# The last five blocks' rows summed on chip, an earlier conditioning piece, and GpSimd on two tiles' gates

## The reference

```python
mod = silu(c) @ w_ada + b_ada                       # 9 rows of 6 pieces of 1024
sh1, sc1, g1, sh2, sc2, g2 = split(mod, 6)
h = x * (1 + sc1) + sh1
z = h @ w_in + b_in                                 # conv, attention, gMLP columns and 3 gates
merged = sig(gA) * A + sig(gB) * B + sig(gC) * C
x = layer_norm(alpha * x + (1 + g1) * (merged @ w_o), ln1_g, ln1_b)
h2 = x * (1 + sc2) + sh2
# 16 experts, top 2 of one group for each token
y = sum(gate[e] * ((silu(h2 @ w_e_gate[e]) * (h2 @ w_e_up[e])) @ w_e_down[e]) for e in chosen)
x = layer_norm(alpha * x + (1 + g2) * y, ln2_g, ln2_b)
```

## Time and profile before

| | us |
|---|---|
| median of three runs | 1091.23 |
| lowest and highest | 1091.19, 1094.38 |
| the profiled execution, its own time | 1096.24 |
| its span in the trace | 1094.1 |
| PE busy | 1001.8 (92%) |
| DVE, POOL, ACT busy | 488.0, 248.1, 189.9 |
| PE busy from 1050.00 to 1094.10 | 0.0 |

### The profile page before, as it was taken

One profiled execution on the slowest core, in us unless ns is written; L12 is line 12 of the kernel. 1 busy time (PEld: TensorE's weight loads), 2 busy tenths in 40 slices (PEclk: granted clock), 3 DMA queues, 4 the chain that ended last, 5 costly groups with the idle time before them and its releaser, 6 DMA issues. The chain is left out here.

```text
span 1094.1 us, 22154 instructions
## 1 busy us (share of the span) xinstructions
PE 1001.8 (92%) x8966; PEld 669.3 (61%) x8966; DVE 488.0 (45%) x1277; ACT 189.9 (17%) x447; POOL 248.1 (23%) x281
## 2 busy tenths in 40 slices
PE   4999999999899999999999999987999999998930
PEld 3777778456676667667777774555655555554510
DVE  2121999973357888855114004677133111110117
ACT  2110112113122213221111110111111111111103
POOL 0000004535121123323335420000212221221133
PEclk8998999999898999999999999987999999999975
DMA  9955645542615205014072308142899899999756
GB/s 298 308 122 149 193 155 173 177 157 89 227 29 157 74 16 193 30 44 121 11 179 71 116 26 331 67 180 100 326 364 378 313 413 388 422 416 419 316 155 125
DMA packets 93732, 214.23 MB, mean 196 GB/s; under 512 B 23464, under 2 KB 48303, under 8 KB 89533
## 3 DMA queue, kind: packets, MB, share of 16 engines
q1 hardware_dynamic: 78388, 186.20, 47.8%
q0 software_dynamic: 6400, 19.01, 5.8%
q10 hardware_dynamic: 8849, 7.64, 2.6%
HBM read 200.46 MB, written 16.92 MB: 199 GB/s over the span
## 5 line engine op out<-in xcount | busy, mean ns | idle before, releaser
L1787 PE MATMUL bank<-arena 128*128 128x288 f32 (+6 forms) x1778 | 445.5, 406 | 8.1 <-DMA arena<-in_w_pa 2.6
L1787 PEld LDWEIGHTS bank<-arena 128*128 128x128 f32 (+2 forms) x1778 | 322.1, 193 | 123.6 <-issue 47.8
L2178 PE MATMUL bank<-arena 128*32 128x256 f32 x3136 | 181.1, 382 | 4.7 <-issue 3.5
L2178 PEld LDWEIGHTS bank<-arena 128*32 128x32 f32 x3136 | 102.3, 109 | 74.8 <-issue 6.7
L1739 DVE TENSOR_TENSOR arena<-arena,bank 128x128 f32<-128x128 f32 x49 | 14.2, 289 | 225.3 <-ACT arena L1176 225.0
L939 POOL DMA_INDIRECT expert_rows<-arena,ints x49 | 47.8, 976 | 224.0 <-ACT arena L1187 224.0
L2197 PE MATMUL bank<-arena 128*32 128x256 f32 x1568 | 94.6, 381 | 0.0
L889 POOL TENSOR_SCALAR arena<-arena 128x288 f32<-128x288 f32 x46 | 43.3, 942 | 212.0 <-ACT arena L1129 212.0
L1249 DVE SCALAR_TENSOR_TENSOR arena<-arena 128x512 f32<-128x512 f32 x120 | 81.9, 742 | 0.0
L1801 PE MATMUL bank<-arena 128*128 128x288 f32 x256 | 69.3, 428 | 2.6 <-DVEq L1267 2.6
L2197 PEld LDWEIGHTS bank<-arena 128*32 128x32 f32 x1568 | 45.9, 108 | 31.8 <-issue 2.0
(11 more groups left out here) (284 smaller groups left out, 888.6 us busy)
## 6 DMA issues: line engine op xcount, KB each, us to landing
arena<-in_w_e_gate SPq DMA_DIRECT2D x16, 2048.0 KB
arena<-in_w_e_up SPq DMA_DIRECT2D x16, 2048.0 KB
arena<-in_w_e_down SPq DMA_DIRECT2D x16, 2048.0 KB
arena<-in_w_ada SPq DMA_DIRECT2D x8, 2048.0 KB, 10.7
arena<-in_w_in SPq DMA_DIRECT2D x8, 2048.0 KB, 10.1
arena<-in_w_ada SPq DMA_DIRECT2D x8, 1024.0 KB, 11.7
arena<-in_x_prompt SPq DMA_DIRECT2D x8, 512.0 KB, 7.1
arena<-in_w_in SPq DMA_DIRECT2D x14, 256.0 KB, 8.2
```

Source lines behind the costliest of these rows:

```text
L1787: last = pe.matmul(out, a, b, start=k == 0, stop=k == len(pairs_) - 1)
L2178: last = pe.matmul(out, HG[:, g % 2, k, a:a + BLK], both_weights(i, k, c), start=k == 0, stop=k == KT - 1)
```

## The change

Three things are done at once. Rows of the last five blocks (44 to 48, `SENT` = 44, `KEPT` = 5) are no longer stored to DRAM and read back: DVE scales them by weight and by the gathered 1 + g2 (`result_up`), and PE sums them into each tile of tokens with one-hot matrices (`OHT`), 20 matmuls for each of the five tiles. GpSimd fetches the gate rows and writes zeros to the five blocks' places meanwhile (`kept_rows`). The other rows are read and paired as soon as they are stored, and gated and added to `X1` apart, tiles 0 to 2 by DVE and tiles 3 and 4 by GpSimd. And conditioning piece 11 stands five steps earlier in the plan. The 1 + g2 is made by a bias in ACT's copy, and two rows fewer are loaded to BC2.

```diff
-    plan += [("lnA1", 2), ("lnA2", 1), ("nat", "u", 4), ("lnA2", 2), ("lnA1", 3), ("mix", 0), ("ada", 11), ("lnA1", 4), ("lnA2", 3), ("mix", 1), ("mix", 2)]
+    plan += [("lnA1", 2), ("lnA2", 1), ("ada", 11), ("nat", "u", 4), ("lnA2", 2), ("lnA1", 3), ("mix", 0), ("lnA1", 4), ("lnA2", 3), ("mix", 1), ("mix", 2)]
...
+        sp.wait_ge(ev("hid_full"), FIRST[NE - 1])
+        sp.wait_ge(ev("g2_in"), 32 * KEPT)
+        for done_ in stored_by(SENT):
+            sp.wait_ge(*done_)
...
+        for t in range(NT):
+            sp.dma_start(GAT[0:rows_of(t), t, :], y_d[t * P:t * P + rows_of(t), :]).then_inc(ev(f"tile_in{t}"), 16)
...
+        def kept_rows(k):
+
+            c = SENT + k
+            pool.indirect_dma_start(G2B[k], None, gates, bass.IndirectOffsetOnAxis(ints[:, I_ROW + c:I_ROW + c + 1], 0)).then_inc(ev("g2_in"), 16)
+            pool.indirect_dma_start(quarters, bass.IndirectOffsetOnAxis(ints[:, I_DEST + c:I_DEST + c + 1], 0), ZERO[:, 0:256], None).then_inc(ev("g2_in"), 16)
...
+        pool.wait_ge(ev("rows2_in"), 64)
+        for t in (3, 4):
+            n = rows_of(t)
+            pool.wait_ge(ev(f"pair_in{t}"), 16)
+            own.link(pool.tensor_tensor(GAT[0:n, t, :], GAT[0:n, t, :], BG2[0 if t < 4 else 1][0:n], ALU.mult))
+            pool.tensor_tensor(X1[0:n, t, :], X1[0:n, t, :], GAT[0:n, t, :], ALU.add).then_inc(ev("pairs_added"), 1)
...
+        def result_up(d):
+
+            if d == SENT:
+                dve.wait_ge(ev("yo_up"), SENT)
+                dve.wait_ge(ev("g2_in"), 32 * KEPT)
+            dve.wait_ge(ev("dn_full"), d + 1)
+            stt(YR[:, yr_of(d), :], banks[6 + d % 2][:, 0:256], WBLK[:, d:d + 1], G2B[d - SENT], ALU.mult, ALU.mult).then_inc(ev("yo_up"), 1)
...
+        for t in range(NT):
+            n = rows_of(t)
+            x, sums, total = X1[0:n, t, :], sum_banks(t), TOTAL[0:n, t:t + 1]
+            if t == 2:
+                pair_gated(t)
+                pair_added(t)
+            if t >= 3:
+                dve.wait_ge(ev("pairs_added"), t - 2)
+            dve.wait_ge(ev("rows_summed"), t + 1)
+            by_quarter = x.rearrange("p (c f) -> p c f", c=4)
+            link(dve.tensor_tensor_reduce(out=by_quarter, in0=by_quarter, in1=sums[0:n], scale=1.0, scalar=0.0, op0=ALU.add, op1=ALU.add, accum_out=total))
+            ts(NMEAN[0:n, t:t + 1], total, -1.0 / (32 * D), None, ALU.mult).then_inc(ev("row_mean"), 1)
...
+            for k in range(KEPT):
+                if t == 0:
+                    pe.wait_ge(ev("yo_up"), SENT + k + 1)
+                for c in range(4):
+                    rows = slice(BLK * c, BLK * c + BLK)
+                    last = pe.matmul(sum_banks(t)[0:n, c, :], OHT[k][rows, t, 0:n], YR[rows, YRS + k, :],
+                                     start=k == 0, stop=k == KEPT - 1)
```

More of the change, by code:

```diff
@@ L52 @@
 NBLK = FIRST[NE]
+SENT = FIRST[NE - 2]
+KEPT = NBLK - SENT
 MIN_CAP = BLK * min(BLOCKS_OF)
@@ L1018, in _ @@
                 for g in range(4):
-                    last = act.activation(mod_buf(n)[:, g * P:g * P + P], mm.tile(key)[32 * g:32 * g + 9, 0:P], ACT.Copy)
+                    last = act.activation(mod_buf(n)[:, g * P:g * P + P], mm.tile(key)[32 * g:32 * g + 9, 0:P], ACT.Copy, bias=1.0 if n >= 10 else 0.0)
                     own.done(last) if g < 3 else last.then_inc(mm.free(key), 1)
@@ L1172, in _ @@
         act.activation(HG[:, 0, 4:8, :], quarter_tiles(banks[4]), ACT.Copy).then_inc(ev("gt_b"), 1)
-        for b in range(NBLK + 2):
-            if b < NBLK:
-                act.wait_ge(ev("hid_full"), b + 1)
-                act.activation(HEB[:, b % 3, :], banks[b % 3][:, gate_half(turn_of[b])], ACT.Silu).then_inc(ev("he_silu"), 1)
+        for b in range(NBLK):
+            act.wait_ge(ev("hid_full"), b + 1)
+            act.activation(HEB[:, b % 3, :], banks[b % 3][:, gate_half(turn_of[b])], ACT.Silu).then_inc(ev("he_silu"), 1)
             if b in tile_behind:
@@ L1199, in _ @@
         each_further(act, nov, further)
+        with act.If(nov > 0):
+            act.wait_ge(ev("row_mean"), 2 * NT)
+            act.wait_ge(ev("less_mean"), 2 * NT)
         for t in range(NT):
@@ L1756, in _ @@
                 spread_up()
+            if b == NBLK - 1:
+                pair_gated(0)
+                pair_added(0)
+            if b == NBLK:
+                pair_gated(1)
+            if b - 2 >= SENT:
+                result_up(b - 2)
+        pair_added(1)
+        for t in range(NT):
+            n = rows_of(t)
+            x, sums, total = X1[0:n, t, :], sum_banks(t), TOTAL[0:n, t:t + 1]
[8 more added lines that the diff above has]
+            ts(NMEAN[0:n, t:t + 1], total, -1.0 / (32 * D), None, ALU.mult).then_inc(ev("row_mean"), 1)
+            link(ts(total, total, -1.0 / D, None, ALU.mult))
+            stt(OUT[0:n, t, :], x, total, BC2[0:n, 0, :], ALU.add, ALU.mult).then_inc(ev("less_mean"), 1)
         nov = dve.value_load(ints[0:1, I_NOV:I_NOV + 1], min_val=0, max_val=NOV)
@@ L2219, in _ @@
                 down(b - 2)
+        pe.wait_ge(ev("he_ready"), NBLK)
+        pe.wait_ge(ev("het_up"), NBLK)
+        for t in range(NT):
+            n = rows_of(t)
+            if t == 1:
+                pe.wait_ge(ev("yo_up"), NBLK)
+            if t >= 2:
+                pe.wait_ge(ev("row_mean"), t - 1)
+            for k in range(KEPT):
+                if t == 0:
+                    pe.wait_ge(ev("yo_up"), SENT + k + 1)
[3 more added lines that the diff above has]
+                                     start=k == 0, stop=k == KEPT - 1)
+            last.then_inc(ev("rows_summed"), 1)
         nov = pe.value_load(ints[0:1, I_NOV:I_NOV + 1], min_val=0, max_val=NOV)
```

237 lines of the change are left out of this document (156 added, 81 removed).

## The result

The changed kernel takes 1085.97 us in the median of 11 runs (1081.02 to 1089.35), the kernel before 1092.68 beside it (11 runs, 1089.47 to 1097.12). The ratio is 0.9928, 95% interval 0.9912 to 0.9944: 7.9 us faster (6.1 to 9.6), where 12.7 were forecast, and 1085.97 where 1078.5 stood. About 1.5 us of that distance are the starting point: the forecast was taken from a median of three runs, 1091.23, which eight more have moved to 1092.68. The profiled execution has a span of 1084.5 us against 1094.1.

A forecast was written before the change was run, and what follows sets the result against it. PE was taken to bound the kernel up to 1050 us, then 44 us of end paced by DVE. Front 6.6 plus end 6.1 gave 12.7 off 1091.23: 1078.5 us, range 1070 to 1084.5.

The forecast's parts named there:

- Front, 6.6 us: First gates: start 3.6 us sooner by the earlier piece 11, plus 3.0 from PE's clock staying up; bounds 0 to 6.6.
- Rival 2: The front gives only its 3.6 us or nothing, through another attention wait or a falling clock: 1081 to 1084.4; chance 0.18.
- When the pairs arrive: Reads of stored rows near the end: first read about 1033.5 us, pair 0 landed at 1046.1, pair 3 at 1053.5.
- The small costs ahead of the end: All 0: Extra short DVE operations, ten more indirect DMAs and one-hot matrices ahead of the end cost nothing; bound 3 us.
- Last blocks: Block 48's down product waits for DVE's copy, held by pair 0: begins at 1049.45, ends at 1051.3, 1.8 us late.
- PE's sums: PE's one-hot sums at the end: 2.3 us a tile with four row groups overlapping; bounds 2.3 to 8.5.
- rival 4: PE's sums do not overlap, 8.5 us a tile; with the front 5.8 us slower, 1097; chance 0.07.
- GpSimd and DVE: GpSimd's work on tiles 3 and 4 collides with DVE's: DVE loses 5.1 us, tile 4's mean at 1073.95.
- Rival 1: GpSimd is no brake, through by 1060: end gives 14.0 us, 20.6 in all, 1070.6; chance 0.18 with values between.
- What is late next: At the end ACT waits for POOL's power of tile 0 until 1070.0; last epsilon 1078.5, DVE's last operation 1079.9.
- End, 6.1 us: DVE's last operation starts at 1079.9 instead of 1085.96, 6.1 us sooner; bounds 3 to 14.0.
- Rival 3: The end gives only 3 us, with pairs at 10.4 and every later power at 1.30: about 1082; chance 0.10.

The follow-up runs named there:

- front_alone: The kernel before with only conditioning piece 11 moved earlier in the plan; 0.9936 of the kernel before, 7.0 us faster.
- end_alone: The changed kernel with conditioning piece 11 put back at its old place in the plan; 0.9979 of the kernel before, 2.3 us faster, not told from nothing.
- Light weights: Changed kernel and kernel before, each loading three quarters of each down matrix from turn 2 on; 0.9875 and 0.9979 of the kernel before.
- small_later: The changed kernel with the kept rows' ten small indirect DMAs issued in blocks 36 to 40 instead of 24 to 28; 0.994 of the kernel before.
- turns_a: The changed kernel with expert turns 2 to 13 in another order; 0.9876 of the kernel before, 13.6 us faster; repeated, 0.9929, 7.8 us.
- dve_gates: The changed kernel with DVE also gating and adding tiles 3 and 4, GpSimd only making powers; 0.9928 of the kernel before.

## Why the prediction was too low

- **Front, 6.6 us: right.** The front part is 607.9 us before and 600.5 after in the profiles (606.4 to 606.8 in the three others with the old plan, 597.1 to 601.5 in the fifteen others with the new), some 6 to 7 us, and `front_alone` is 7.0 faster. That "the whole train moves" held up to the first flip, and in the median of `front_alone` to the end. Rival 2 (the front gives only a part) is out.
- **The failed step: "When the pairs arrive", and with it "PE waits for no expert weights at all".** Pair 0 was to land at 1046.1, 0.55 us behind the last flip. It is used 1.7 behind it in the changed kernel, 3.9 to 5.7 in the five other runs with kept rows, full weights and the old turns, since its reads, 17 us sooner than before against that flip, meet the last of a full stream of weights. The offsets of the earlier trace rows were measured with DMA engines at a share of 0.13. In `end_alone` the store took 5.62 us instead of 3.39 and the first read 8.11 instead of 3.28, and pair 0 came 5.1 later than forecast; from its use to DVE's last operation it took 34.4 us, where the forecast had 35.1. So in that profile the date of the pairs is the whole of what the end fell short by (4.5 us). The row of `hidden` said "issue 3.5"; in the changed kernel that pause ends with a weight's landing. Light weights gave the second half 5.4 us instead of 2.1 in the profiles; in the medians the change went from 7.9 to 11.4, which is within the noise.
- **"The small costs ahead of the end: All 0", bound 3 us: wrong in the blocks themselves, right for the stage in the old order of turns.** The ten transfers go into a full stream: in eight of fourteen profiles PE's blocks beside them are 3.8 to 5.3 us longer in all. That they are the cause is supported by the blocks' place, by their absence without kept rows and by `small_later`, and not shown; by what way they slow PE is open. In the old order the loss near 990 is then gone, so that the stage is not longer for it. In the order of `turns_a`, which has no loss there, it adds: 294.7 us without long blocks and 299.4 with them.
- **Last blocks:** down(48) was late by 2.7 us instead of 1.8, the same late pair.
- **PE's sums: right**, 2.26 us a tile (2.3); rival 4 is out. The last one took 4.27 at half clock, for which no term stood; DVE waited 0.41.
- **GpSimd and DVE: right.** In the changed kernel four DVE operations were held by 0.49, 0.60, 2.13 and 2.02 us over 1.28 and 1.23 alone, 5.2 in all (5.1), which speaks for an exclusive turn at SBUF as the Trainium skill's "SBUF — State Buffer", Who interferes with whom, has it, also in that the operation with one input from PSUM (1.22) was not held. Rival 1 is out. The consequence that I did not draw is that the moved work, 4.9 us, is then worth little: `dve_gates` puts it at 0.5 us against `end_alone`.
- **What is late next: right in kind** (ACT waited 7.41 for a power) but mis-sized: later powers took 0.56 us and not 1.30, so ACT caught up, and DVE's last tile, not ACT's loop, ended last.
- **End, 6.1 us:** 7.2 in the one profile, where PE's pause let the pairs be nearly on time; 1.6 in `end_alone`, whose median is 2.3 below the kernel before. So 7.2 is luck of that execution. Rival 3 (the end gives only 3) describes the median, though its reasons, pairs at 10.4 us and slow powers, are not what the runs show.
- No step spoke of the clock's second fall near 758 (between 752 and 762 in the others). It is there in eleven of sixteen profiles with the new plan, `front_alone` among them, and in none of the four with the old one. The same eleven have 9.5 to 10.05 us for the first hidden products, the nine others 8.4 to 8.65. Where both come together they cost some 3 us; the medians hold them already. Whether the earlier piece brings them about is open.

## What to carry to other kernels

Offsets from issue to landing hold for the load under which they were read: ask what the DMA share is at the new date before moving a read to it. A pause named "issue" on an engine that streams weights is to be held against the landing of the transfer that it needs next. And before work goes to an idle engine, see whether its operations take turns with those that they are to relieve. A transfer that delays an engine is not yet a loss, if that engine waits for the same stream of weights later on.

## What was not expected of the hardware

Behind ten microseconds with a DMA share of 0.97 to 1.01, 5.7 to 8.7 us passed from the issue of the first read of a pair to that of the second, which waits for it, against 3.9 to 4.1 with a share of 0.12 to 0.16. PE stopped inside one product for 0.3 to 0.8 us beside indirect DMAs of GpSimd, waiting for nothing that the trace shows. One kernel, measured in two sets of runs, came out 13.6 and 7.8 us below the kernel before, a difference larger than either half interval (3.5 and 2.6 us).
